# One more column chunk in the first pass of a fused transformer block: the 336-column chunk of the input projection

## The reference, cut to what matters

```python
mod = silu(c) @ ada_w + ada_b              # 2048 x 12288; six segments of 2048
sh_a, sc_a, g_a, sh_f, sc_f, g_f = split(mod, 6)
h = rms_norm(x, attn_pre_g) * (1 + sc_a) + sh_a
proj = h @ w_in                            # q | kv | g_nsa | c_q | c_kv | k_r | g_merge
y = token_mixer(...)                       # compressed, selected and window attention (NSA),
                                           # latent attention (MLA), gates, two output projections
x = x + g_a * rms_norm(y, attn_post_g)
h = rms_norm(x, ffn_pre_g) * (1 + sc_f) + sh_f
x = x + g_f * rms_norm(peer_ffn(h), ffn_post_g)   # top-k experts, rows gathered from u and v
```

## Time and profile before

| | |
|---|---|
| median of three runs | 2202.79 us (2201.09 to 2204.48) |
| the profiled execution's own time | 2193.92 us |
| its span | 2192.2 us, 15905 instructions |
| busy: TensorE, VectorE, ScalarE, GpSimd | 88%, 53%, 17%, 35% of the span |
| moved by DMA | 825.44 MB, 377 GB/s in the mean |

### The profile page before, as it was taken

One profiled execution on the slowest core, in us unless ns is written; L12 is line 12 of the kernel. 1 busy time (PEld: TensorE's weight loads), 2 busy tenths in 40 slices (PEclk: granted clock), 3 DMA queues, 4 the chain that ended last, 5 costly groups with the idle time before them and its releaser, 6 DMA issues.

```text
span 2192.2 us, 15905 instructions
## 1 busy us (share of the span) xinstructions
PE 1919.8 (88%) x5155; PEld 895.0 (41%) x5155; DVE 1151.2 (53%) x2052; ACT 369.4 (17%) x961; POOL 772.3 (35%) x708
## 2 busy tenths in 40 slices
PE   3899999999999989999899898997778778778687
PEld 2445654444444445555334333443333333333233
DVE  6757367622113366777444346436564654655643
ACT  2001011221301133345000012111201101101101
POOL 4312111100000256666422135226554454464452
PEclk7899999999999999999999999999988889889889
DMA  9998889965597899999999999999999999999996
GB/s 364 390 371 315 289 286 391 374 237 157 169 356 277 300 422 421 419 421 421 418 417 417 418 417 420 417 418 421 421 423 418 422 416 422 422 422 422 422 422 287
DMA packets 164056, 825.44 MB, mean 377 GB/s; under 512 B 17156, under 2 KB 23528, under 8 KB 88724
## 3 DMA queue, kind: packets, MB, share of 16 engines
q0 software_dynamic: 92160, 637.58, 70.7%
q1 hardware_dynamic: 70084, 186.28, 23.6%
q10 hardware_dynamic: 1744, 0.73, 0.1%
HBM read 822.40 MB, written 2.13 MB: 376 GB/s over the span
## 4 chain that ended last, share of the span: by engine, by line
PE 54%; DMA 38%; DVE 3%; issue 2%; POOL 1%; ACT 1%; SPq 0%; DVEq 0%; POOLq 0%; ACTq 0%
DMA arena<-in_peer_v_dram,idx_now 20%; PE PS L1098 15%; PE PS L1589 12%; PE PS L1547 10%; PE PS L1504 9%; DMA arena<-in_w_out_dram 5%; DMA arena<-in_ada_w_dram 4%; DMA arena<-in_w_branch_mla_dram 3%; DMA arena<-in_peer_w_q_dram 3%; DMA arena<-in_w_branch_nsa_dram 2%; DMA arena<-in_peer_u_dram,idx_now 2%; DVE arena L1658 1%; PE PS L1474 1%; PE PS L1275 1%; PE PS L1146 1%
## 5 line engine op out<-in xcount | busy, mean ns | idle before, releaser
L1589 PE MATMUL PS<-arena 128*128 128x512 f32 x1024 | 492.4, 645 | 139.3 <-DMA arena<-in_peer_v_dram,idx_now 138.0
L630 POOL DMA_INDIRECT arena<-in_peer_v_dram,idx_now x256 | 361.0, 1410 | 587.1 <-PE PS L1547 339.3
L1547 PE MATMUL PS<-arena 128*128 128x512 f32 x1024 | 469.9, 603 | 31.2 <-DMA arena<-in_peer_v_dram,idx_now 28.3
L2148 DVE CUSTOM_DVE_ANT_0 arena<-arena 128x2048 f32<-128x2048 f32 x128 | 291.9, 2292 | 254.3 <-DMA arena<-in_peer_u_dram,idx_now 254.2
L2122 DVE CUSTOM_DVE_ANT_0 arena<-arena 128x2048 f32<-128x2048 f32 x128 | 292.6, 2290 | 198.2 <-DMA arena<-in_peer_u_dram,idx_now 195.6
L1589 PEld LDWEIGHTS PS<-arena 128*128 128x128 f32 x1024 | 210.7, 208 | 421.0 <-issue 389.9
L1098 PE MATMUL PS<-arena 128*128 128x512 f32 (+1 forms) x848 | 364.1, 582 | 1.0 <-ACT arena L738 1.0
L630 POOL DMA_INDIRECT arena<-in_peer_u_dram,idx_now x256 | 305.7, 1194 | 151.7 <-issue 70.7
L1504 PE MATMUL PS<-arena 128*128 128x512 f32 x688 | 319.1, 603 | 33.0 <-DMA arena<-in_w_out_dram 13.6
L1547 PEld LDWEIGHTS PS<-arena 128*128 128x128 f32 x1024 | 191.1, 193 | 262.9 <-issue 219.3
L1098 PEld LDWEIGHTS PS<-arena 128*128 128x128 f32 x848 | 158.3, 190 | 172.0 <-issue 163.2
(11 more groups left out here) (271 smaller groups left out, 1133.8 us busy)
## 6 DMA issues: line engine op xcount, KB each, us to landing
arena<-in_ada_w_dram POOLq DMA_DIRECT2D x64, 1024.0 KB, 8.0
arena<-in_w_in_dram SPq DMA_DIRECT2D x112, 512.0 KB, 7.1
arena<-in_ada_w_dram POOLq DMA_DIRECT2D x64, 512.0 KB, 10.6
arena<-in_w_out_dram SPq DMA_DIRECT2D x64, 512.0 KB, 10.9
arena<-in_peer_w_q_dram SPq DMA_DIRECT2D x64, 512.0 KB, 9.9
arena<-in_w_branch_nsa_dram SPq DMA_DIRECT2D x32, 512.0 KB, 9.7
arena<-in_w_branch_mla_dram SPq DMA_DIRECT2D x32, 512.0 KB, 10.9
arena<-mod_rows SPq DMA_DIRECT2D x7, 1024.0 KB, 16.5
```

Of the source, the lines that this page charges most:

```text
L630: pool.indirect_dma_start(dst, None, tab, bass.IndirectOffsetOnAxis(ap=idx_now[:, now, e:e + 1], axis=0)).then_inc(landed, 16)
L1547: ins = nc.tensor.matmul(PS[:, k, :], diag[i % 8], Vrow0[i % RING0][:, k * NC:(k + 1) * NC], start=(i == 0), stop=False, skip_group_check= ...
L1589: ins = nc.tensor.matmul(PS[:, 4 + k, :], diag[e % 8], Vrow[e % RING][:, k * NC:(k + 1) * NC], start=(first and e == 0), stop=False, skip_ ...
L2148: v.tensor_tensor_reduce(row, row, h2[1], 1.0, 0.0, ALU.mult, ALU.add, dots[:, e:e + 1]).then_inc(u_free, 1)
```

## The change

The tail chunk joins the first pass. The pass has four equal steps as before (`STEPS`, four column blocks each), but eight tiles in a step: two of C0 and C1 together, one of C2, one of the tail, for every pair of blocks. Its accumulators take banks 6 and 7, and the column sums move to columns 480 to 511 of bank 6. VectorE makes each piece of `ada_w` in two operations of 1024 columns into one accumulator, each behind the one before it, where it had four of 512. POOL's two loads of a piece are split by segment and no longer by row. The tail is copied out by ScalarE at the end of the pass, and it leaves its old place before the transposes of Q.

Behind the pass, the column sums of the third segment come before the products of the compression (bank 3); C5 stands in two halves around the compression's second layer and half of the key transposes; gate chunk 0 stands in three parts (two tiles, two tiles, four tiles) around the transposes of Q and the compressed scores. VectorE has rows 0 to 7 before the rotation of K, 8 to 11 after it, then 12 to 15, `mod_out(0)`, the rotation of Q, rows 16 to 19, the compression's copies, rows 20 and 21, and rows 22 and 23 after the copies of K. `ADA_NSA` becomes 24, so none stands after the compressed probabilities, and the last eight come with the first four MLA units. POOL loads rows 12 to 15 before its copies of V.

```diff
-        QTRS, FIRST_TILES = D // NC, 24
-        MOD_BANK, ADA_NSA = (1, 5, 5, 5), 2 * KD - 4
+        QTRS, FIRST_TILES = D // NC, 2 * KD
+        STEPS = ((0, 4), (4, 4), (8, 4), (12, 4))
+        MOD_BANK, MOD_COL, ADA_NSA = (3, 5, 5, 5), NC - 2 * KD, 2 * KD - 8
-        W_C3, W_C4, W_CMP, W_C5, W_TAIL = 24, 32, 40, 48, 56
-        W_QUP = W_TAIL + 8 + 5 * 8
+        W_C3, W_C4, W_CMP, W_C5, W_G0 = 32, 40, 48, 56, 64
+        W_QUP = W_G0 + 5 * 8
...
+        def first_acc(q):
+            c0, n = q % 2 * 2 * NC, STEPS[q][1] * P
+            return acc[:, c0:c0 + 2 * n]
+
+        ADA_FIRST = [(q, j, 4 * 2 // s) for q, (k0, s) in enumerate(STEPS) for j in range(0, KD, 4 * 2 // s)]
...
         def first_tile(m):
-            k4, i = 4 * (m // 6), m % 6
-            return (k4 + 2 * (i // 3), 2) if i % 3 == 2 else (k4 + i // 3 * 2 + i % 3, 1)
+            k2, i = 2 * (m // 4), m % 4
+            return (k2, i) if i >= 2 else (k2 + i, 1)
...
+                elif n == 3:
+                    load(m, win_v[:, k:k + 2, TAIL0:GM0], TAIL)
...
-            load_chunk(W_TAIL, TAIL0, TAIL)
...  (POOL)
+                q, j, rows_ = ADA_FIRST[n]
+                for seg in range(2):
+                    c0 = seg * D + k0 * P
+                    pool.dma_start(place[:, :, seg, :], ada_v[:, j:j + rows_, c0:c0 + s * P]).then_inc(
+                        ada_in[n % ADA_SLOTS], 16)
...
+            for r in range(12, KD):
+                ada_row(r)
             pool.wait_ge(pj_out, 3)
             pool.wait_ge(cmpx_ready, 2)
...
-            for r in range(12, KD + 8):
+            for r in range(KD, KD + 8):
                 ada_row(r)
...  (ScalarE)
+            chunk_out(3, FIRST_TILES, lambda t: proj[:, t, TAIL0:GM0], pj_out, 6)
...
-            main_out(5, W_C5 + 8)
             act.wait_ge(ada_used, ROW0 + KD)
             for j in (0, 2):
                 act.wait_ge(kT_in, j + 1)
...
+                if j == 0:
+                    main_out(5, W_C5 + 8)
...  (TensorE)
+            for q, (kq, s) in enumerate(STEPS):
+                pe.wait_ge(ada_used, 2 * (kq + s))
...
+                for m in range(2 * kq, 2 * (kq + s)):
...
+                            kk, bank = (k0 + i, 2 * n + t) if n >= 2 else (k0, 2 * i + t)
+                            cols = TAIL if n == 3 else NC
...
             chunk(0, W_C4, hT, KD)
+            pe.wait_ge(pj_out, 5)
+            column_sums(0)
...
-            pe.wait_ge(pj_out, 5)
-            column_sums(0)
-            chunk(2, W_C5, hT, KD)
+            pe.wait_ge(mod_ready, 1)
+            chunk(2, W_C5, hT, KD, part=range(4))
...
                 if j == 2:
+                    chunk(2, W_C5, hT, KD, part=range(4, 8))
                     pe.wait_ge(cmpkv_ready, 2)
...
-            chunk(0, W_TAIL, hT, KD, TAIL)
...
+                if j % 2:
+                    chunk(0, gate_tile(0), hT, KD, part=range(j - 1, j + 1))
...
-            chunk(2, gate_tile(0), hT, KD)
+            chunk(0, gate_tile(0), hT, KD, part=range(4, 8))
...
-                if n in (2, 10):
+                if n in (4, 12):
                     column_sums(1 + n // 8)
...  (VectorE)
-            for r in range(4):
+            for r in range(8):
                 ada_row(r)
...
-            for r in range(4, 8):
+            for r in range(8, 12):
                 ada_row(r)
...
-            for r in range(8, KD):
+            for r in range(12, KD):
+                ada_row(r)
+            mod_out(0)
+            dve.wait_ge(pj_out, 6)
+            dve.wait_ge(rope_ready, 3)
+            rope(Q0, HEADS, q_roped)
+            for r in range(KD, KD + 4):
                 ada_row(r)
...
-            for r in range(KD + 6, ADA_NSA):
-                ada_row(r)
```

More of the change, by code:

```diff
@@ L797, in _ @@
             act.wait_ge(lat_in, 3)
-            nc.scalar.copy(ckvT.rearrange("p j t -> p (j t)"), PS[:, 0, :]).then_inc(lat_act, 1)
+            nc.scalar.copy(ckvT.rearrange("p j t -> p (j t)"), PS[:, 2, :]).then_inc(lat_act, 1)
             act.wait_ge(pct_in, 1)
@@ L1100, in products, with chunk @@
                 return ins
-            def chunk(bank, m, lhs, ktiles, cols=NC):
-                for w in range(ktiles // 2):
+            def chunk(bank, m, lhs, ktiles, cols=NC, part=None):
+                for w in part or range(ktiles // 2):
                     tile_ready(m + w)
@@ L1667, in reduced @@
+            modulate(len(STEPS) - 1)
             def reduced(r, k):
@@ L1771, in _ @@
                 ins.then_inc(cmprep_ready, 1)
-            mod_out(0)
-            dve.wait_ge(pj_out, 5)
-            dve.wait_ge(rope_ready, 3)
-            rope(Q0, HEADS, q_roped)
-            for r in range(KD, KD + 4):
+            for r in range(KD + 4, KD + 6):
                 ada_row(r)
@@ L1790, in _ @@
                               PS[:, (6, 7, 4, 5)[j], :]).then_inc(kT_dve, 1)
-            for r in range(KD + 4, KD + 6):
+            for r in range(KD + 6, ADA_NSA):
                 ada_row(r)
```

102 lines of the change are left out of this document (44 added, 58 removed).

## The result

The changed kernel takes 2182.56 us (median of 4 executions, 2181.45 to 2183.65) beside 2201.94 us for the kernel before: a ratio of 0.991, 95% interval 0.9893 to 0.9927, or 19.4 us less. Two later groups gave 2183.13 and 2183.22 us (4 executions each, ratios 0.9907 and 0.9908). The forecast was 13.4 us less, 2189.4, and its range began at 2184.0: the direction and the places were right, the size was not, and the result lies 1.4 us outside the range.

A forecast was written before the change was run, and what follows sets the result against it. The pass was taken as bound by transfers, the fillers by TensorE, the join by VectorE behind loads. 8.3 - 18.1 - 0.9 - 2.7 = -13.4 us, from the median 2202.8, gave 2189.4 us; range 2184 to 2196.

The forecast's parts named there:

- the sum: Whole kernel: pass +8.3, tail off TensorE's path -18.1, gate chunk parts -0.9, join -2.7, together -13.4 us.
- Part 1, the pass: First pass: taking in the tail's tiles and products makes it end at 166.8, not 158.55, +8.3 us.
- The first step: First step of the pass: one tail tile replaces a full one, so it ends 0.3 us earlier, at 41.1.
- The rival of TensorE as the pass's bound: First pass: TensorE at clock 0.83 sets every step, pass +18.1 us, total 2199 us; chance 0.13.
- Tail tiles: Loads of the pass: each 344 KB tail tile costs 1.10 us, against 0.91 by the Trainium skill.
- Part 2, the walk through the waits: Fillers between pass and attention: tail gone -18.1, gate chunk parts -0.9 us; new order adds no waits, row slack 5.5 us.
- Part 3, the join: Before the attention: with no row ahead of VectorE's last copies it starts at about 316.9, not 319.57, -2.7 us.
- NSA and MLA: Stages after the attention's start: NSA neither gains nor loses; four rows moved to MLA units 2 and 3 cost nothing.
- rivals of late rows: Third segment: rows 8 to 15 come late and hold up its column sums, total 2209 us; chance 0.07.
- the MLA stage giving it back: MLA units 2 and 3: four row operations delay the softmax steps by up to 9.8 us, 2199 us; chance 0.07.
- the gate chunk's parts: Fillers before the attention: three parts of gate chunk 0 cover the wait for the Q copies, -0.9 us.
- from the profile to the median: Whole kernel: the saving reckoned from a 2193.92 us profiled execution was subtracted unchanged from the 2202.8 us median.

The follow-up runs named there:

- wider tail tiles: The changed kernel with the tail's tiles loaded 512 columns wide, of which 336 are still used: 2185.17 us.
- join undone: The changed kernel with rows 22 to 27 put back behind the compressed probabilities, before the attention: 2199.66 us.
- products in the join: The kernel before with three unread 512-column products on TensorE while it waits for VectorE ahead of the attention: 2198.49 us.
- join alone: The kernel before with only rows 22 to 27 moved from before the attention, two to rows 20 and 21, four to MLA units: 2194.16 us.
- fillers in one piece: The changed kernel with C5 undivided and gate chunk 0 undivided behind the compressed scores: 2192.12 us.
- four operations: The changed kernel with each `ada_w` piece again in four 512-column operations on two accumulators in turn: 2180.50 us, again 2180.67 us.

## Where the prediction was right, and where it was wrong

**Right, the sum, as the traces measure it.** Before the attention the profiles give 319.8 - 305.8 = 14.0 us. Behind it the changed kernel takes 1.3 us more in the mean (1876.7 us from the attention to the end in three profiles, 1875.3 in four before), which is less than those four differ among themselves (1872.6 to 1879.5). That is 12.7 us between profiled executions, against 13.4 forecast. Some of this closeness is luck: the pass cost 1.9 us less than forecast, the rest up to the attention gave 1.3 us less, and the two misses nearly cancel.

- *Part 1, the pass.* Forecast +8.3. C3 starts at 158.5 in the mean of four profiles before and at 164.8 in three after: +6.4, the good end of the range. The last sums stood at 136.4 (136.7 in the mean of three), as forecast, though TensorE and not the loads set that, and their products took 25.36 us and not 27.0. The forecast carried over the 22.5 us of the old third step, at a clock of 0.94, with 0.42 us of idle time before its sums and 2.70 behind them; the new last step has none before them and 1.06 behind. The rule of the Trainium skill that the text set against the row (TensorE: Matmul & The Clock Gate, Part 1: activity releases the throttle) gives what these traces show, 1.00 in the whole last step; the trace of the wider tail tiles, at 0.51 from 143 to 146 in a step with equally little idle time, shows that this is not sure.
- *The first step.* The forecast let it end 0.3 us earlier, at 41.1. The sums stand at 39.2 in all three profiles of the changed kernel and at 40.9 to 42.0 in the four before. Four operations per piece leave them there (39.1 and 39.5), so the merged operations are not the reason. Up to the sums SyncE's queue moved 4.58 MB where it had moved 4.92, which at the 2.64 us per MB of the sum is 0.9 us; the rest is open. The steps behind it grew by more than forecast instead.
- *The rival of TensorE as the pass's bound* did arise in part. TensorE comes last at the end of the first and of the third of the stretches above, and in both the clock was 0.84, where the rival had 0.83; they took 32.7 and 32.8 us, where the rival had 33.5. It did not hold for every step: the second had 1.00 and a wait for the loads at its end, the last 1.00, so that 28.1 us were enough for it.
- *Tail tiles.* The forecast took 1.10 us for one over the 0.91 that the line rate of the Trainium skill gives (DMA: Bandwidth & Descriptors, Specifications). The pass, tail rows of 1344 B included, runs at 390 GB/s, no slower than before, which is as the rule says. SyncE's queue in the first full step shows 32.4% for 3.88 MB:

```profile
q1 hardware_dynamic: 1673, 3.88, 32.4%
```

  over 32.2 us, or 2.69 us per MB, where full tiles alone had 2.64; 3.88 MB are about six full and two tail tiles, which would be 2.74 with the 3.21 of the earlier trace rows. The row alone doesn't decide. The 3.21 came from a stretch where the DMA share was 0.82 and TensorE was busy without a break, so it was a doubtful price for a stretch at 1.03.
- *Part 2, the walk through the waits.* No wait arose. The sums of the third segment stood at 221.24 (223.5 forecast), with 8.3 us of slack and not 5.5. From C3 to the attention the profiles give 161.3 before and 140.9 after, 20.4 us less where parts 2 and 3 have 21.7. Most of the missing 1.3 us is in the two later profiles of the changed kernel, where the half chunk behind the compressed scores took 15.68 us and not 13.98. TensorE's timeline of the second:

```profile
288.64 15.68 PE L1108 MATMUL PS<-arena 128*128 128x512 f32 x32
```

- *Part 3, the join.* TensorE's wait before the attention was 3.1 us in the mean and is 1.1: 2.0 us less, where the term had 2.7. VectorE still releases the attention, which the prediction had named as a sign of being wrong; but no row stands before that copy any more.
- *NSA and MLA.* Both as forecast, unchanged at 268.8 us together. The rivals of late rows and of the MLA stage giving it back are refuted by that and by the slack.

**Right as terms of the sum, wrong as prices of the edits: the gate chunk's parts and the join.** The text put the parts of the gate chunk at -0.9 and the join at -2.7, each as a correction of its own. Counted from the old order that is what the traces show, within a microsecond. But undone in the changed kernel they cost 9 us and 16.5 us. The sum was not hurt by it, since it took both for done. It hid what the change rests on. Of two paths that end together, the gain of one is worth only what the other allows: with all the rest of the change and the old join, the time is 2199.66. The lesson of the gate chunk is the same: its price must be read with what the *new* order puts ahead of the awaited copies, two rows, and with the clock behind the idle time.

**Wrong, and the step that failed: from the profile to the median.** "Everything behind the attention's start moves with it", and the 8.9 us by which the profiled execution lay below the median were carried over to the changed kernel as a constant: 2202.8 - 13.4. They were not one. The four profiled executions of the kernel before have a mean of 2196.9 us, 4.5 below its median of 2201.4, and the first, from which the forecast was made, lay 7.5 below; the three of the changed kernel have a mean of 2184.2, 1.1 above the mean of its twelve executions. So by the medians the change is worth 18 to 19 us and by the profiles 12.7, and it is this difference of 5 to 6 us, put at nothing without a reason, that the forecast lacks. Had the 13.4 us been subtracted from the profiled execution, the result would have been 2180.5; the median was 2182.56. By groups:

```
kernel                          executions   median    mean granted   its profiled executions
                                             us        clock
with rows at the join
  before                        66           2201.4    0.9439         2193.92 2200.24 2198.33 2195.04
  join undone in the change     11           2199.66   0.9428         2198.02
  products in the join          12           2198.49   0.9445         2194.25
without
  join alone                    8            2194.16   0.9462         2193.27
  fillers in one piece          9            2192.12   0.9459         2192.36
  wider tail tiles              6            2185.17   0.9455         2183.33
  changed, second               4            2183.13   0.9470         2186.29
  changed, third                4            2183.22   0.9468         2184.73
  four operations               4            2180.50   0.9467         2180.10
  four operations, again        4            2180.67   0.9485         2182.42
```

All six profiled executions of kernels with rows at the join lie below their kernel's median, by 1 to 8 us; those of the others lie on both sides. And over all executions the granted clock of the first three is lower, 0.943 to 0.9445 against 0.9455 to 0.9485. Within the 66 executions of the kernel before it goes with the time too: 0.9447 in the faster half (mean 2198.5 us), 0.9432 in the slower (2203.8), and 0.9458 in its four profiled ones. A difference of 0.002 in the mean, over 2200 us, is some 9 us more at the lower of the two levels, or about 4.5 us of time where TensorE is the bound. That is near the 5 to 6 us that the medians show and the traces don't, but it is an estimate, and a lower clock can be the effect of waiting as well as the cause of a longer time. It doesn't say where, either: in the first profile before, the clock is 1.00 over the NSA and MLA stages and 0.94 over the expert phase, far behind the join. And products in the idle time of the join left the mean clock at 0.9445. So this much is shown: most of the extra goes with the edit of the join (join alone: 7.0 us by the medians, 2.0 to 2.4 at the join in its trace). That edit does more than clear the join: it moves four rows to the MLA units and closes two segments two NSA units later, and no run separates these. Where in the execution the extra is lost, and why, stays open: four profiles of the kernel before did not catch it.

The range shared the fault. Its lower end, 16.5 us and the scatter below the median, had no case in which that offset changes, though 8.9 us was more than any term but the tail's.

## What to carry to other kernels

Where two engines' paths end within a few microseconds of each other at a join, price an edit on both: most of the larger saving is worth nothing until the smaller wait goes (1.5 us of 18 by the medians here), and neither term can be added on its own. Read the price of a cover from what the new order puts behind it, and add the clock behind the idle time that is left bare, where it falls. Before a difference between two traces is put down to an edit, subtract what the two already differ by ahead of it: 1.8 of the 4.2 us of the join alone were that. When a profiled execution is far from the median of its kernel, ask what that distance consists of and whether the change touches it, and widen the range by it on the side where it could vanish.

## What the runs showed that was not expected

- Idle time of TensorE can cost more than its length, and by its length one can't tell. 4.78 us of it made the work behind it 4.7 us longer (fillers in one piece), 14.46 us made it 1.8 us longer (join undone), 2.35 us 1.7 us longer, and 2.81 to 3.82 us nothing (the four profiles of the kernel before): what counts is how much work the lower clock catches. It comes without idle time too: behind the 32-column products of the compressed scores, with no gap, the half chunk took 1.7 us longer in two profiles of the changed kernel out of three.
- TensorE's lag moves transfers. SyncE's queue and VectorE in the changed kernel, end of the third step:

```profile
134.31 2.64 SPq L429 DMA_DIRECT2D arena<-in_w_in_dram  x2
```

```profile
129.78 2.60 DVE L1669 SCALAR_TENSOR_TENSOR arena<-arena,csil 128x1024 f32<-128x1024 f32 x2 [1.44 <-DMA arena<-in_ada_w_dram]
138.25 0.16 DVE L1651 TENSOR_TENSOR arena<-PS,arena 128x4 f32<-128x4 f32 x1 [5.86 <-PE PS L1145]
```

  The last piece of `ada_w` is done at 132.4, 4 us before TensorE asks for it (the forecast had it in at 136.6), and SyncE, which waits for TensorE's count, issues two of its weight tiles only at 134.31. That the weights held back left the `ada_w` pieces more of the bandwidth would explain it, but no run here tests it.
- A chain of two operations of 1024 columns per piece, against four of 512 on two accumulators, is 2.4 us slower in the means, though VectorE has a third of each step free. No trace here shows where.
